# The first block of input weights in two transfers, and the products of two token tiles split to match

## What is computed

```python
def mixer_inputs(x, g, w_in, b_gates):
    h = rms_norm(x, g).astype(x.dtype)
    p = h @ w_in                       # 1024 x 3080
    mq, mk, mv, mo, mi, mf, dq, dk, dv = jnp.split(p, split_points(), axis=-1)
    ...
```

## Time and profile before

| what | value |
|---|---|
| median of 3 runs | 688.2 us (687.59 to 917.83) |
| the profiled execution's own time | 685.39 us |
| its span in the profile | 683.6 us |
| PE busy | 621.6 us (91%) |
| PE's share of the chain that ended last | 60% |
| DMA's share of that chain | 21% |

### The profile page before, as it was taken

The page is one execution under the profiler, slowest core; times in us unless marked ns, Lnnn a source line. Parts: engine busy times, 40 slices in busy tenths (PEclk is TensorE's granted clock), DMA queues, the critical chain, the costliest instruction groups (busy, mean ns, idle before and its releaser), DMA issues.

```text
span 683.6 us, 8735 instructions
## 1 busy us (share of the span) xinstructions
PE 621.6 (91%) x3207; PEld 336.8 (49%) x3207; DVE 285.8 (42%) x647; ACT 139.3 (20%) x409; POOL 118.6 (17%) x206
## 2 busy tenths in 40 slices
PE   4999999899999999999989996999999878999791
PEld 3444444444544565455545573655555444555440
DVE  3220058433334352669788766523212211112066
ACT  3110141333332454310131100110010000100022
POOL 2340006120040111101021201012321111120013
PEclk9999999999999999999999965999999998999996
DMA  9725247833030300043873699999999999999993
GB/s 293 224 82 176 55 164 203 274 117 124 1 109 16 123 1 1 0 124 81 238 328 134 213 392 369 352 418 421 417 400 418 421 420 420 424 417 423 416 361 129
DMA packets 59409, 165.76 MB, mean 242 GB/s; under 512 B 18345, under 2 KB 27866, under 8 KB 46694
## 3 DMA queue, kind: packets, MB, share of 16 engines
q1 hardware_dynamic: 49590, 147.97, 56.7%
q0 software_dynamic: 7552, 17.19, 7.6%
q10 hardware_dynamic: 2224, 0.04, 0.2%
HBM read 150.88 MB, written 23.34 MB: 255 GB/s over the span
## 4 chain that ended last, share of the span: by engine, by line
PE 60%; DMA 21%; DVE 6%; SPq 5%; issue 3%; ACT 3%; POOL 1%; DVEq 0%; ACTq 0%; POOLq 0%
PE bank L2015 12%; DMA WS<-in_w_down_e 9%; PE bank L2233 9%; PE bank L2012 7%; PE bank_p L2285 4%; DMA FT<-in_w_up_e 4%; PE scores L2298 3%; PE bank_t L2285 3%; SPq L581 2%; DMA WS<-out_rows 2%; PE bank_t L2029 2%; DMA MO<-in_cache_k,pages 2%; PE bank_p L2138 2%; DMA WS<-in_w_in 2%; PE scores L2155 1%
## 5 line engine op out<-in xcount | busy, mean ns | idle before, releaser
L2015 PE MATMUL bank<-WS,XHT 128*128 128x512 f32 x192 | 88.9, 610 | 2.2 <-DMA WS<-in_w_in 1.6
L2012 PE MATMUL bank<-XHT,WS 128*128 128x512 f32 x192 | 85.0, 597 | 0.6 <-PE bank_t L2029 0.6
L2015 PEld LDWEIGHTS bank<-WS,XHT 128*128 128x128 f32 x192 | 35.5, 193 | 43.7 <-issue 41.3
L2012 PEld LDWEIGHTS bank<-XHT,WS 128*128 128x128 f32 x192 | 35.7, 190 | 42.9 <-issue 42.7
L2285 PE MATMUL bank_p<-WS,XHT 128*64 128x256 f32 x288 | 45.5, 391 | 5.1 <-issue 1.7
L2285 PE MATMUL bank_t<-WS,XHT 128*64 128x256 f32 x288 | 43.0, 381 | 1.7 <-DMA FT<-in_w_up_e 1.5
L967 POOL DMA_INDIRECT out_rows<-MVA,slot_ids x15 | 15.1, 1008 | 159.7 <-DVE MVA L1825 159.7
L2285 PEld LDWEIGHTS bank_p<-WS,XHT 128*64 128x64 f32 x288 | 27.8, 141 | 19.6 <-issue 5.0
L2285 PEld LDWEIGHTS bank_t<-WS,XHT 128*64 128x64 f32 x288 | 27.2, 137 | 14.9 <-DMA FT<-in_w_up_e 2.0
L854 POOL TENSOR_SCALAR rr<-ss 128x1 f32<-128x1 f32 (+3 forms) x25 | 7.2, 287 | 150.6 <-ACT XHT L1226 43.0
L1825 DVE COPY MVA<-scores 128x512 f32<-128x512 f32 x16 | 11.1, 693 | 50.3 <-PE scores L2298 50.3
(11 more groups left out here) (473 smaller groups left out, 1052.5 us busy)
## 6 DMA issues: line engine op xcount, KB each, us to landing
WS<-in_w_gate_e SPq DMA_DIRECT2D x16, 1024.0 KB, 19.5
WS<-in_w_up_e SPq DMA_DIRECT2D x16, 1024.0 KB, 22.3
WS<-in_w_down_e SPq DMA_DIRECT2D x16, 1024.0 KB, 25.9
WS<-in_w_in SPq DMA_DIRECT2D x6, 2048.0 KB, 10.4
XHT<-in_w_gate_e SPq DMA_DIRECT2D x10, 1024.0 KB, 24.6
XHT<-in_w_up_e SPq DMA_DIRECT2D x10, 1024.0 KB, 25.9
XHT<-in_w_down_e SPq DMA_DIRECT2D x10, 1024.0 KB, 28.2
FT<-in_w_gate_e SPq DMA_DIRECT2D x6, 1024.0 KB, 23.0
```

Of the source, the lines that this page charges most:

```text
L2012: mm = pe.matmul(PS[r][:, :], w[:, k, 128 * m:128 * (m + 1)], hT[:, k, 0:512], start=(k == 0), stop=(k == KC - 1))
L2015: mm = pe.matmul(PS[r][:, :], hT[:, k, 128 * m:128 * (m + 1)], w[:, k, :], start=(k == 0), stop=(k == KC - 1))
```

## The change

`schedule()` puts two new items behind the first two transposes: the first four slices of the products of tiles 0 and 1 with block `dv`. The items `("acc", "dv", 0)` and `("acc", "dv", 1)` keep the other four. Block 0 is loaded by two transfers of 1024 KB, slices 0 to 3 and slices 4 to 7, each with its own semaphore (`head_in`, `block_in[0]`). To have a semaphore for it, `dr_zeroed` and `ident_made` are made one, which counts to 2.

```diff
-    order = [("xt", 0), ("xt", 1)]
+    order = [("xt", 0), ("xt", 1), ("pre", "dv", 0), ("pre", "dv", 1)]
...
-                sp.dma_start(blkslot[n % 3], src).then_inc(block_in[n % 3], 16)
+                if n == 0:
+                    sp.dma_start(blkslot[0][:, 0:4], src[:, 0:4]).then_inc(head_in, 16)
+                rest = slice(4 if n == 0 else 0, KC)
+                sp.dma_start(blkslot[n % 3][:, rest], src[:, rest]).then_inc(block_in[n % 3], 16)
...
-            sp.wait_ge(dr_zeroed, 1)
+            sp.wait_ge(dr_ident_made, 1)
...
-            pool.nop().then_inc(dr_zeroed, 1)
+            pool.nop().then_inc(dr_ident_made, 1)
...
-            pool.nop().then_inc(ident_made, 1)
+            pool.nop().then_inc(dr_ident_made, 1)
...
-            act.wait_ge(ident_made, 1)
+            act.wait_ge(dr_ident_made, 2)
...
-                        pe.wait_ge(ident_made, 1)
+                        pe.wait_ge(dr_ident_made, 2)
...
-                    if m == 0 and kind != "post":
+                    if m == 0 and b == "dv":
+                        pe.wait_ge(*((head_in, 16) if kind == "pre" else (block_in[0], 16)))
+                    elif m == 0 and kind != "post":
```

More of the change, by code:

```diff
@@ L348, in build @@
         const_in, const_made, pad_zeroed = sem("const_in"), sem("const_made"), sem("pad_zeroed")
-        gmix_in, ident_made, dr_zeroed, wg_zeroed = sem("gmix_in"), sem("ident_made"), sem("dr_zeroed"), sem("wg_zeroed")
+        gmix_in, dr_ident_made, head_in, wg_zeroed = sem("gmix_in"), sem("dr_ident_made"), sem("block_head_in"), sem("wg_zeroed")
         gfin_in = sem("gfin_in")
```

## The result

The changed kernel took 693.18 us in the median of 22 runs (687.24 to 741.14), the kernel before, timed beside it, 688.95 (22 runs). The ratio is 1.0057, with a 95% interval of 1.0034 to 1.0079: slower by 3.9 us (2.3 to 5.4). The difference is within two per cent, as forecast, but the interval excludes a ratio of 1, and the median lies above the range of 686.2 to 691.0. The profiled execution took 693.57 us, its span is 691.8.

What follows compares the result with a forecast made beforehand. PE was taken to bound the kernel, busy 621.6 us. A 1.77 us earlier start became idle time before DVE's copy of tile 1, net +0.43, so 688.2 + 0.43 = 688.6 us; range 686.2 to 691.0.

Steps and rivals of the forecast that it cites:

- PE at 10.96: Tile 0's first half-product starts at 10.96 instead of 12.73, after DVE's copy of tile 0: 1.77 us gained.
- My 18.26 assumes that it wakes fast from that: PE resumes at 18.26, 0.15 us after DVE's copy of tile 1, at full speed despite 0.4 to 2.1 us idle.
- The sum: PE's work from 18.26 to tile 3's transposes: 6.87 + 0.88 + 3.44 = 11.19 us, ending at 29.45.
- rival (a): Matmuls behind PE's pause run at a lower clock: price 1.4 to 1.7 us, total +2.1, 690.3 us; chance 0.24.
- The term of 0.43: Net cost at the start of tile 3's transposes: 29.45 instead of 29.02, so 0.43 us slower.
- Rival (d): Tile 2's rows land later by a gap between block 0's halves: +1.4 (689.6) or +2.4 (690.6); chance 0.12.
- 2.0 us per transfer: Skill's fixed time per DMA; as queue time, tile 2's rows land 2.0 us later, cost 2.4; chance 0.03.
- the boundary between the halves: Queue gap between block 0's two transfers: taken as 0, with 1.0 us kept for the range.
- (b): Longer slow start at 12.73 in the kernel before, hidden in the changed one: -1.3 us, 686.9; chance 0.15.
- (c): DVE's copy of tile 1 ends near 12.5, so PE saves the whole 1.77 us: 686.4; chance 0.05.
- (e): Block 0's first half lands no sooner, both near 12.7; time stays the forecast's; counted in its chance of 0.44.
- I carry 0.43 in full: Stages after the first stretch have no fixed time, so the 0.43 us reaches the end undiminished.

Runs made afterwards that it cites:

- e3: Changed kernel with block 0 loaded in one transfer, new product order kept; ratio 1.0011 to the kernel before.
- e4: Changed kernel with only tile 0's product split, no half-product of tile 1 up front; ratio 0.9944 to the kernel before.
- e5: Changed kernel with DVE copying tile 1 before it scales tile 2; ratio 0.9965 to the kernel before.
- e12: Changed kernel with tile 2's rows loaded between the two halves of block 0; ratio 0.9970 to the kernel before.
- the late table: Changed kernel with GpSimd's page-table load issued after POOL's five roots; ratio 0.9970 to the kernel before.
- e2: Changed kernel with block 0 still in two transfers but products in the old order, the first waiting for both halves; ratio 1.0000 to the kernel before.
- e1: Changed kernel run again, no edit; ratio 1.0045 to the kernel before.
- e10: Changed kernel run again on another chip, no edit; ratio 1.0067 to the kernel before.
- e13: Changed kernel run again on another chip, no edit; ratio 1.0042 to the kernel before.
- e15: Kernel before with GpSimd's page-table load issued after POOL's five roots; ratio 1.0044 to the unedited kernel before.
- e14: Changed kernel with GpSimd's page-table load issued after POOL's five roots, second run; ratio 0.9992 to the kernel before.
- the filler: Changed kernel with unused products of tile 0 put into PE's pause, run twice; ratios 1.0016 and 1.0056 to the kernel before.
- e11: Changed kernel with unused products of tile 0 in PE's pause, second run; ratio 1.0056 to the kernel before.
- e16: Kernel before profiled again, no edit, one execution; 688.67 us.
- e9: Kernel before run again, no edit; ratio 1.0011 to the kernel before.

## Why the prediction was wrong, point by point

**The mechanism was right, its size was not.** PE at 10.96, idle ahead of tile 1's half-product, released by DVE's copy, and the copy's chain: all as forecast. e3, e4, e5 and e12, each of which takes the pause away by another edit, measured 1.0011, 0.9944, 0.9965 and 0.9970. The forecast gave +0.43 us, the measurement +3.9.

**The step that failed is "My 18.26 assumes that it wakes fast from that".** The sum gives the sixteen matmuls behind the pause 6.87 us; in four of six profiles they took 8.38 to 8.67. It is my rival (a), "PE wakes slowly", which I gave 0.24. I wrote that the pause has dense matmuls on both sides and that "half of it or more may vanish if the first eight run slow". The two term sizes behind it: a forecast pause of 0.4 to 2.1 us, against 2.51 to 4.04 measured. The first eight matmuls took 3.99 to 4.83 us; I had allowed 5.1 to 6.8, taking the slow start of the kernel before over to a stream that follows transposes without a gap. The sooner they are done the longer PE stands idle, as the end of the pause is set by DVE. The pauses of 3.03, 3.32, 3.86 and 4.04 us were followed by slow matmuls, and 2.94 with the late table; those of 1.81, 2.51 and 2.79 were not, against my "it decides from a pause near 2 us". The rule that I cited from the Trainium skill, "TensorE: Matmul & The Clock Gate", section "HAM oscillation", agreed with the traces more than I let it: a wait between short bursts did put PE back to half rate (granted clock 0.54).

**The baseline.** The profile of before was an early one: block 0 at 12.73, against 13.26 and 13.46 in two others, rows of tile 2 at 14.00 against 14.56 and 14.96. Both kernels' terms move with the same landing, so this hardly changes the difference: by the means, 14.51 + (18.11 - 14.00) + 0.15 + 11.19 = 29.96 against 29.51 gives +0.45. The term of 0.43 stands.

**The sum as measured.** At the comparison point the mean difference is 1.69 us: 0.45, plus 0.15 for the rows, plus slow matmuls, 4/6 of some 1.6 us = 1.1.

**Rival (d), and 2.0 us per transfer.** I took 0 for the boundary between the halves. e2 speaks against a cost in the time (ratio 1.0000), but the rows landed at 14.38 to 16.28 in eleven profiles with two transfers and the early table, mean 15.09, and at 14.00 to 14.96 in four with one, mean 14.49. The ranges overlap; the slices of 6 to 7 us do not (see e2), and by their bytes the queue is 0.2 us behind. So the term is a few tenths. The 2.0 us per transfer that the prediction takes from the Trainium skill ("DMA: Bandwidth & Descriptors", section "Anatomy of one DMA") are not in the means, which differ by 0.6; the latest single landing (e2) is 1.8 behind the mean of one transfer.

**Rivals (b), (c) and (e).** (c) was made true by e5 and gave its sign. (e) was nearly e3. (b), that the kernel before starts slower in other executions, did not come about: it has about four slow matmuls in all three profiles.

**How the range failed.** I let each case stand alone and ended the range at the single most expensive one. They add up: rows that land late lengthen the pause, and a longer pause is followed by slow matmuls. But the first stretch as measured (1.69) lies inside what rival (a) alone allowed (2.1), and even (a) and (d) together would give 691.3. Of the 4.6 us between 688.6 and 693.18, 0.75 are the kernel before, which had 688.95 in 22 runs and not 688.2, 1.3 are the first stretch beyond 0.43, and some 2.5 are what follows.

**What stays open.** The four timed comparisons of the changed kernel say +2.9 to +4.6 us, and the first stretch accounts for about 1.7. The sentence "I carry 0.43 in full" holds up to 114 us, where the difference arrives within 0.03 us, and behind the stop the profiles of the changed kernel are rather shorter (0.6). So some 2 us more are in executions that were not profiled, or at the stop. Two things speak for the former in part: the profiles without slow matmuls are of fast executions, and typical ones, at 31.6 to 32.4, are 2.1 to 2.9 behind.

The granted clock is on record for every timed execution, as a mean over its span. Read as time at 1.2 GHz with the rest at 2.4, the means over the executions that the ratios use (27 to 31 of the kernel before, 8 to 12 of the changed one) give this estimate:

| executions on one chip | mean granted clock | us at 1.2 GHz, before | changed | ratio of changed |
|---|---|---|---|---|
| e1 | 0.9626 before, 0.9592 changed | 51.0 | 55.9 | 1.0045 |
| e10 | 0.9634 before, 0.9576 changed | 49.9 | 58.1 | 1.0067 |
| e13 | 0.9607 before, 0.9573 changed | 54.0 | 58.9 | 1.0042 |

That is 4.9 to 8.2 us more at the lower clock, which cost PE at most half of it, 2.5 to 4.1 us, of a loss of 2.9 to 4.6. One slow stretch behind the pause is some 3.4 us at that clock, so more of it must lie elsewhere, and the profiles don't show where. Beside e1 the kernels without a pause have 49.4 (e2), 50.1 (e3) and 49.2 (e4), as the kernel before; the control e15 has 57.6 against 54.0, which is up to 1.8 of its 3 us. It is no proof: a stop can itself let the clock fall, and e14 has 57.8 with a ratio of 0.9992. Against the clock as the whole answer stands the filler too: its two profiles have no slow stretch, are 1.1 behind at the comparison point, and its times say +1.1 and +3.8 us (e11: 52.8 us at 1.2 GHz). Something besides may belong to the loss. The cause of the stop near 120 us was not found.

## What to carry to other kernels

Before an item is moved ahead on one engine, follow what it waits for on the others, down to their program order: the half-product of tile 1 was not held by its weights but by a copy that stood, on DVE, behind work on rows of another tile. Split only as far as the operands are there; the first half of tile 0's product alone gave 0.9944, and with tile 1's added it was 1.0045 on the same chip. And where TensorE is given an early start, ask how long it will then stand idle: here the sixteen matmuls behind pauses of 3.03 us and more took 1.4 to 1.7 us longer than the 6.97 behind the shorter ones.

## What the runs showed of the hardware that I had not expected

- Sixteen packets of 512 B from GpSimd's queue, the page table for all partitions, stand beside a dip of the hardware queue to 22 to 56 GB/s over a microsecond. Loaded late, the same slice carried 264 to 274 with block 0 in two transfers, but 135 with block 0 in one, and there the bytes up to 9 us stayed the same.
- A matmul stream that followed the transposes without a gap reached full speed sooner (the first eight in 3.99 to 4.83 us) than one that started after 1.6 us of waiting (sixteen in 8.54 us, four of them slow, so the first eight in about 5.1).
- Slow matmuls don't always show in the granted clock: with four at half speed behind the wait for block 0 it reads 1.00 in the profile before and in e16 (13.4 to 16.8 us), and 0.62 in e9 (13.2 to 16.7).
- Unaltered, the same kernel's landing of one 2 MB block differs by 0.7 us from execution to execution (12.73 to 13.46), its whole span by 3.6 us (683.6 and 687.2), and a stop of 3.3 us at 120 us may or may not be there; eight profiles on two chips have none. One profile is one draw.
